# Inverting the delta rule's triangular blocks as 64x64 tiles, with the outer blocks in the last level and one modulation vector in the recurrence

## The reference, cut to what matters

```python
def gated_delta_chunked(q, k, v, beta, g):
    G = jnp.cumsum(gc, axis=-1)
    L = jnp.exp(jnp.where(incl, G[..., :, None] - G[..., None, :], -jnp.inf))
    kb = kc * bc[..., None]
    A = jnp.where(strict, jnp.einsum('bnhtd,bnhsd->bnhts', kb, kc) * L, 0.0)
    T = lax.linalg.triangular_solve(eye + A, eye, left_side=True, lower=True, unit_diagonal=True)
    U = T @ (vc * bc[..., None])
    W = T @ (kb * jnp.exp(G)[..., None])
    qk = jnp.where(incl, jnp.einsum('bnhtd,bnhsd->bnhts', qc, kc) * L, 0.0)

    def step(state, inp):
        v_new = u - w @ state
        o = qd @ state + qkc @ v_new
        state = gl[..., None, None] * state + jnp.swapaxes(kd, -1, -2) @ v_new
        return state, o
```

## Time and profile before

| | |
|---|---|
| median of three runs | 3473.8 us |
| the profiled execution | 3486.42 us, span 3484.6 us |
| TensorE busy (matmuls) | 3113.0 us, 89% |
| VectorE busy | 1155.4 us, 33% |
| ScalarE busy | 896.8 us, 26% |
| delta rule of layer 0 | 320.9 to 468.9 us |
| delta rule of layer 1 | 1177.6 to 1327.1 us |

### The profile page before, as it was taken

The page is one execution under the profiler, slowest core; times in us unless marked ns, Lnnn a source line. Parts: engine busy times, 40 slices in busy tenths (PEclk is TensorE's granted clock), DMA queues, the critical chain, the costliest instruction groups (busy, mean ns, idle before and its releaser), DMA issues. The chain is left out here.

```text
span 3484.6 us, 39509 instructions
## 1 busy us (share of the span) xinstructions
PE 3113.0 (89%) x17446; PEld 2112.2 (61%) x17446; DVE 1155.4 (33%) x1616; ACT 896.8 (26%) x1354; POOL 0.2 (0%) x4
## 2 busy tenths in 40 slices
PE   5997889999898788999989998879899985999997
PEld 3775767888676576788867766644343352443442
DVE  3446533233445653323343236630000136100002
ACT  3443223222444312322243350220000032100001
POOL 0000000000000000000000000000000000000000
PEclk8997989999999798999999999889999997999999
DMA  7224312322223411232363106249999952799996
GB/s 256 80 90 147 97 37 85 97 91 91 76 85 109 168 39 40 93 97 91 100 216 122 37 3 240 73 152 404 409 408 409 409 193 93 301 409 409 409 408 242
DMA packets 247386, 637.14 MB, mean 183 GB/s; under 512 B 12848, under 2 KB 110128, under 8 KB 247088
## 3 DMA queue, kind: packets, MB, share of 16 engines
q1 hardware_dynamic: 244128, 627.22, 48.4%
q10 hardware_dynamic: 3088, 7.40, 0.6%
HBM read 632.48 MB, written 2.10 MB: 182 GB/s over the span
## 5 line engine op out<-in xcount | busy, mean ns | idle before, releaser
L609 PE MATMUL ps<-mix_halves,work_halves 128*128 128x512 f32 (+1 forms) x1544 | 623.5, 404 | 39.5 <-DVE h_halves L2095 30.3
L609 PE MATMUL ps<-h_halves,work_halves 128*128 128x512 f32 (+1 forms) x1544 | 610.1, 395 | 4.6 <-DVE mix_halves L2095 2.4
L609 PE MATMUL ps<-mix_halves,ring_halves 128*128 128x512 f32 x1448 | 568.1, 392 | 0.0
L2095 DVE TENSOR_TENSOR ring_halves<-ring,work_halves 128x2048 fp32r<-128x2048 f32 (+2 forms) x125 | 252.6, 2021 | 546.2 <-ACT work_halves L1488 449.3
L609 PE MATMUL ps<-ring,work 128*64 128x512 f32 x1680 | 389.4, 594 | 22.3 <-DMA ring<-in_w_exp_gate 18.3
L609 PEld LDWEIGHTS ps<-mix_halves,work_halves 128*128 128x128 f32 (+1 forms) x1544 | 291.8, 189 | 126.7 <-issue 42.6
L609 PEld LDWEIGHTS ps<-h_halves,work_halves 128*128 128x128 f32 (+1 forms) x1544 | 292.5, 189 | 72.5 <-issue 6.4
L609 PEld LDWEIGHTS ps<-mix_halves,ring_halves 128*128 128x128 f32 x1448 | 272.3, 188 | 60.7
L1488 ACT ACTIVATE work_halves<-ring 128x2048 fp32r<-128x2048 f32 x102 | 188.3, 1846 | 425.6 <-PE ps L609 333.2
L609 PEld LDWEIGHTS ps<-ring,work 128*64 128x64 f32 x1680 | 128.0, 137 | 256.0 <-issue 255.6
L2474 DVE SCALAR_TENSOR_TENSOR x<-ps,small,x 128x512 f32<-128x512 f32 x112 | 82.3, 750 | 594.3 <-PE ps L609 592.8
(11 more groups left out here) (371 smaller groups left out, 3349.3 us busy)
## 6 DMA issues: line engine op xcount, KB each, us to landing
ring<-in_w_exp_gate SPq DMA_DIRECT2D x114, 1024.0 KB, 11.3
ring<-in_w_exp_down SPq DMA_DIRECT2D x100, 1024.0 KB, 12.8
ring<-in_w_exp_up SPq DMA_DIRECT2D x96, 1024.0 KB, 15.1
ring<-in_ada_w SPq DMA_DIRECT2D x48, 1024.0 KB, 7.4
ring<-in_w_mod SPq DMA_DIRECT2D x48, 1024.0 KB, 7.5
proj<-in_w_exp_up SPq DMA_DIRECT2D x28, 1024.0 KB, 12.8
proj<-in_w_exp_down SPq DMA_DIRECT2D x28, 1024.0 KB, 16.0
ring<-in_w_in SPq DMA_DIRECT2D x22, 1024.0 KB, 5.4
```

The lines of the kernel that those rows point to most:

```text
L609: i = pe.matmul(o, lhsT, rhs, start=start, stop=stop, **kw)
L2095: to("lo", tt(rounded(v), v, rounded(hi), ALU.subtract))
```

## The change

The 16 matrices are cut into 64x64 blocks. Only the diagonal ones are inverted by levels: the upper left blocks lie in partitions 0 to 63 and the lower right ones in partitions 64 to 127 of the same columns (`g_Ac`, `g_Tc`, `g_Yc`, `g_Xc`, 16 blocks side by side, 1024 elements to a partition where there were 2048). A product of a level is now 32 products of 64x64 by 64 columns, alternately in the upper left and the lower right quarter of the array (`products`). There are five full levels, up to blocks of 64. The last level forms the outer block alone from the right half of A (`g_Ar`): X = A T of the upper left inverse, 16 products, and X^T Y, 16 products. VectorE lays the result out as the full `g_Y` that the recurrence reads. Signals, copies and subtractions go by half (8 blocks) and no longer by head, each with 512 elements to a partition. The masks come from `b_mask`, 64 wide, left by the stage before. ScalarE has a new copy of the lower diagonal blocks (`g_diag`). Turning Y is now a product with the identity.

Modulation vector 5 moves into the recurrence: two panels after chunk 0, two after chunk 1, its turn after chunk 2, VectorE's `columns_out` after the loop.

```diff
@@ TensorE, delta
-                for i in (4, 5):
-                    for first in (0, 2):
-                        mod_panels(PLANS[f"layer{l}"], i, first, i, (4,))
+                for first in (0, 2):
+                    mod_panels(PLANS[f"layer{l}"], 4, first, 4, (4,))
                 pe.wait_ge(*due("g_y"))
...
+                def products(bank, lhs, rhs, half, signal):
+                    for g in blocks(half):
+                        for r in (lower, upper):
+                            mm(at_block(r, bank, g), lhs[r, g, :], rhs[r, g, :], True, True,
+                               signal if g % 8 == 7 and r is upper else None)
...
+                for n in range(len(LEVELS) - 2):
                     for half in range(2):
                         pe.wait_ge(*due("g_al"))
+                        if n:
+                            pe.wait_ge(*due("g_tt"))
+                        products(0, g_al[n % 2], g_Tc, half, "g_x")
                     if n == 0:
-                        pe.wait_ge(*due("mod_ready", 2))
+                        pe.wait_ge(*due("gn"))
+                        pe.wait_ge(*due("mod_ready"))
                     for half in range(2):
+                        pe.wait_ge(*due("g_x_sb"))
+                        if n:
+                            pe.wait_ge(*due("g_yt"))
+                        products(6, g_Yc, g_Xc, half, "g_dt")
+                        products(4, g_Xc, g_Yc, half, "g_dy")
+                for half in range(2):
+                    pe.wait_ge(*due("g_tt"))
+                    for g in blocks(half):
+                        mm(at_block(upper, 0, g), g_Ar[lower, g, :], g_Tc[lower, g, :], True, True,
+                           "g_x" if g % 8 == 7 else None)
+                for half in range(2):
+                    pe.wait_ge(*due("g_x_sb"))
+                    pe.wait_ge(*due("g_yt"))
+                    for g in blocks(half):
+                        mm(at_block(lower, 4, g), g_Xc[upper, g, :], g_Yc[upper, g, :], True, True,
+                           "g_dy" if g % 8 == 7 else None)
...
+                    if c < 2:
+                        mod_panels(PLANS[f"layer{l}"], 5, 2 * c, 5)
+                    if c == 2:
+                        mod_turn(5, 5)
@@ ScalarE, delta
+                act.wait_ge(*due("g_acc", 2))
+                to("g_diag", f(g_Ac[64:P, :, :], g_Ar[64:P, :, :], ACT.Copy))
...
+                for _ in LEVELS[1:-1]:
+                    for half in range(2):
+                        copy_half("g_x", g_Xc, half)
+                for half in range(2):
+                    copy_half("g_x", g_Xc, half, slice(64, P))
@@ VectorE, delta
+                for half in range(2):
+                    dve.wait_ge(*due("g_score", 2))
+                    s, d = (by_halves(v[:, 2 * half:2 * half + 2, :]) for v in (ps, g_L))
+                    tt(g_Ac[0:64, eight_of(half), :], s[0:64, :, 0, :], d[0:64, :, 0, :], ALU.mult)
+                    to("g_acc", tt(g_Ar[:, eight_of(half), :], s[:, :, 1, :], d[:, :, 1, :], ALU.mult))
...
-                link(tt(by16(g_A), by16(g_A), const("below").unsqueeze(1).to_broadcast([P, 16, P]), ALU.mult))
-                link(tt(by16(g_Y), by16(g_A), table(first_t, "level1").unsqueeze(1).to_broadcast([P, 16, P]), ALU.mult))
-                to("g_y", tt(by16(g_Y), ident.unsqueeze(1).to_broadcast([P, 16, P]), by16(g_Y), ALU.subtract))
+                dve.wait_ge(*due("g_diag"))
+                link(tt(g_Yc, g_Ac, b_mask[:, 6:7, :].to_broadcast([P, 16, 64]), ALU.mult))
+                to("g_y", tt(g_Yc, b_mask[:, 0:1, :].to_broadcast([P, 16, 64]), g_Yc, ALU.subtract))
...
+                dve.tensor_copy(g_Yq[0:64, :, 0, :], g_Yc[0:64, :, :])
+                dve.tensor_copy(g_Yq[64:P, :, 1, :], g_Yc[64:P, :, :])
+                for half in range(2):
+                    dve.wait_ge(*due("g_dy"))
+                    to("g_yt", ts(g_Yq[0:64, eight_of(half), 1, :], change(4, half)[0:64, :, :], -1.0, None, ALU.mult))
...
                 due("g_state")
+                columns_out(PLANS[f"layer{l}"], 5, 5)
                 coefficients(l)
```

More of the change, by code:

```diff
@@ L247 @@
     "g_kb": "VectorE: k beta", "g_k": "TensorE: k by tokens", "g_k_sb": "ScalarE: in SBUF",
+    "g_diag": "ScalarE: the lower diagonal blocks beside the upper ones",
     "g_score": "TensorE: a head's products", "g_acc": "VectorE: with decay", "g_y": "VectorE: the first level's inverse",
@@ L381, in build @@
         b_s, b_tmp = cut(work, 5120, 256, b=2, e=P), cut(work, 5376, 256, b=2, e=P)
-        g_A, g_T, g_Y = (four(work, 2048 * i) for i in range(3))
-        g_X = four(proj_all, 2048)
+        g_Ac, g_Ar, g_Tc, g_Yc = (cut(work, 1024 * i, 1024, g=16, t=64) for i in range(4))
+        g_Xc, g_Y = cut(proj_all, 2048, 1024, g=16, t=64), four(work, 4096)
+        g_Yq = g_Y.rearrange("p h (c u t) -> p (h c) u t", u=2, t=64)
         g_vt, g_kdt = cut(proj_all, 4096, 1024, c=4, f=256), cut(proj_all, 5120, 1024, c=4, f=256)
@@ L387, in build @@
         g_qk, g_L = four(hbuf, 0), four(hbuf, 2048)
-        g_al = (four(proj_all, 0), g_L)
-        g_eg = two(proj_all, 0)
+        g_al = (cut(proj_all, 3072, 1024, g=16, t=64), cut(hbuf, 2048, 1024, g=16, t=64))
+        g_eg = two(proj_all, 1024)
         g_s = cut(work, 7168, 256, b=2, e=P)
@@ L964, in delta @@
                 pe.wait_ge(*due("g_k_sb"))
-                for i in (4, 5):
-                    for first in (0, 2):
-                        mod_panels(PLANS[f"layer{l}"], i, first, i, (4,))
+                for first in (0, 2):
+                    mod_panels(PLANS[f"layer{l}"], 4, first, 4, (4,))
                 pe.wait_ge(*due("g_y"))
-                for hd in range(H1):
-                    for c in range(NT):
-                        turn(ps[:, hd, c * P:c * P + P], g_Y[:, hd, c * P:c * P + P], "g_t" if c == NT - 1 else None)
+                lower, upper = slice(0, 64), slice(64, P)
@@ new lines, in at_block, with blocks @@
+                def at_block(rows, bank, g):
+                    return ps[rows, bank + g // 8, g % 8 * 64:g % 8 * 64 + 64]
+                def blocks(half):
+                    return range(8 * half, 8 * half + 8)
+                def products(bank, lhs, rhs, half, signal):
[3 more added lines that the diff above has]
+                               signal if g % 8 == 7 and r is upper else None)
@@ L972, in delta @@
+                for g in range(16):
+                    for r in (lower, upper):
+                        t = pe.matmul(at_block(r, 0, g), g_Yc[r, g, :], ident[r, r], start=True, stop=True)
+                        if g % 8 == 7 and r is upper:
+                            t.then_inc(sem["g_t"], 1)
                 mod_turn(4, 4)
-                mod_turn(5, 5)
-                pe.wait_ge(*due("g_t_sb", H1))
-                for n, s in enumerate(reversed(LEVELS[:-1])):
-                    last = s == LEVELS[0]
+                pe.wait_ge(*due("g_t_sb", 2))
@@ L996, in delta @@
-                        if not last:
-                            if n == half == 0:
-                                pe.wait_ge(*due("gn"))
-                            for hd in (2 * half, 2 * half + 1):
-                                if half:
-                                    pe.wait_ge(*due("g_tt"))
-                                for c in range(NT):
-                                    cs = slice(c * P, c * P + P)
-                                    mm(ps[:, 6 + hd % 2, cs], g_Y[:, hd, cs], g_X[:, hd, cs], True, True,
-                                       "g_dt" if c == NT - 1 else None)
@@ L1006, in delta @@
-                    pe.wait_ge(*due("g_yt", 2))
-                    if not last:
-                        pe.wait_ge(*due("g_tt", 2))
+                        pe.wait_ge(*due("g_x_sb"))
[8 more added lines that the diff above has]
+                           "g_x" if g % 8 == 7 else None)
@@ L1742, in delta @@
                         split_panel()
+                    if c == 2:
+                        row_out(5, 5)
+                act.wait_ge(*due("mod_tr", 6))
                 act.wait_ge(*due("g_ds", NT))
@@ L2347, in hc @@
                     return v.rearrange("p (h c) -> p h c", c=4)
+                dve.memset(g_Yq[64:P, :, 0, :], 0.0)
                 dve.wait_ge(*due("g_gates_sb"))
```

79 lines of the change are left out of this document (33 added, 46 removed).

## The result

The changed kernel takes 3375.4 us (median of four executions, 3371.2 to 3381.4) against 3477.2 of the kernel before beside it: a ratio of 0.971, 95% interval 0.969 to 0.973. The forecast was 3432.0. The time lies inside the range given, 3372 to 3444, but the gain is more than twice what the likeliest case had; it is the first rival's case, *full clock*, which was put at 3379 with a chance of 0.24.

The account below looks back on a forecast made before the run. TensorE was taken to bound the kernel, with VectorE binding at the front of the two changed stages. Terms -5.1, -5.1, -14.2, -0.7 and +4.2 gave -20.9 us a layer, -41.8 for two: 3432.0 us, range 3372 to 3444.

Parts of the forecast that it names:

- the likeliest case: Levels start at clock 0.50 and stay there until the recurrence: -20.9 us a layer, 3432.0 us in all, chance 0.60.
- full clock: Rival: two quarters at once suffice for clock 1.00, a middle level takes 5.75 us; -47.3 us a layer, 3379 us; chance 0.24.
- burst: Half a level product, 32 instructions of 64x64 by 64: 0.94 us at clock 1.00, 1.71 us at 0.50.
- pairing: In the levels' products, two opposite quarters of the array work at once; doubted because both write one PSUM bank.
- The clock: From the gap before the first level until the recurrence, granted clock 0.50, a level taking 10.3 us.
- Front: Before the first X^T Y: fewer and smaller VectorE mask and block operations, after waiting for two heads; -5.1 us a layer.
- First level: From the first X^T Y: 11.9 us becomes four halves at 1.71, 6.8 us; -5.1 us a layer.
- four levels: Middle levels: 55.4 us becomes 41.2, at 10.3 a level, with no other engine binding; -14.2 us a layer.
- Last level: Four single-quarter bursts at 1.71 us plus latency, negation and clearing: 8.96 us becomes 8.2; -0.7 us a layer.
- Recurrence: Vector 5's panels lengthen two chunks and the start is at clock 0.50: +4.2 us a layer, between +1 and +7.
- Cost nothing there: At the front, before the change, vector 5's panels stood under VectorE's masks and cost no time.
- No pairing: Rival: hardware takes the quarters in turn, a level takes 20.5 us; +26.8 us a layer, 3527 us; chance 0.08.

Follow-up runs that it names:

- the kernel with one row half: Changed kernel, but both blocks of each pair in the middle levels' products take the lower rows and go to the two column halves by turns: 3412.8 us, ratio 0.981.
- one row half after the other: Changed kernel, but in each half product of the middle levels all eight lower-row blocks stand first, then all eight upper-row blocks: 3471.8 us, ratio 0.998.

## Why the prediction was wrong

- *What bounds the kernel, burst, pairing.* Right. A half product is 0.93 us at 1.00 (0.94 forecast) and 1.71 at 0.50, the figure forecast, measured in the kernel with one row half. Two readings were off. That "no row of this trace has opposite quarters at once" is wrong: the burst at 270.80 goes to all four quarters in turn and has 64 instructions in 1.16 us, so pairing deserved less doubt. And "next to no traffic: 58 GB/s" is a mean over the stage: from 342.9 to 362.7 us the loads run at 254 GB/s, and it is behind such loads that TensorE later paused.
- *The clock: the step that failed.* "A fully busy TensorE does not by itself bring the clock back" held, 78 busy us at 0.50. "One that addresses half of its array did not" was read wrongly off: those 64-row blocks lack half of the rows (eight instructions in one row half, then eight in the other for the next head), and I carried it over to two quarters as a half of the *area*. Two opposite quarters lack nothing of the rows. The kernels above part the two: one row half 0.50 for 53 us, one row half after the other 0.50 for 78 us, both row halves by turns back at 1.00 after 3.4 us. The levels took 5.8 us in place of 10.3. The sentence for the rival, that alternating quarters keep all rows in turn, was the mechanism, and it got 0.24.
- *Front* -5.4 for -5.1: right, by the same operations (the 0.55 us of waiting for two heads in the forecast's sum lie ahead of where the table starts; like for like it is -5.4 for -5.65). *First level* -6.9 and *four levels* -32.2 for -5.1 and -14.2: all the clock's. No other engine binds. *Last level* -3.8 for -0.7, likewise: 5.1 us, at 1.00.
- *Recurrence* +0.7 in layer 0 and -4.1 in layer 1 for +4.2: the sign of the move was wrong, too. The +4.2 doesn't follow from its own terms: 1.4, 2.1 and 1 are 4.5 before "a bit less than another slow chunk" is added. The first chunk came as priced, 10.6 us (8.53 and 2.1). But the 7.12 us that the sum took for a chunk at full clock has a slow stretch in it, the row below; at 1.00 a chunk without panels takes 5.76 us.

```profile
441.80:445.10 3.30, 3.14 (x20) 2.52 (x20) 0.65 (x2) 1.46 (x3) 0.00 (x0) 0.50 0.00 0
```

- *The panels in it* cost 0.6 us a chunk at 1.00 (6.4 against 5.8 of the third), but with them the clock stays up for longer; alone, the move makes the recurrence 3.2 and 4.5 us shorter. "Cost nothing there" was also incomplete: at the front the panels, used up early, pull loads into the levels. The kernel before had loads there too (352 GB/s in its first level) and no such pause; it used up a packet of instructions in 16 to 20 us, the changed one in 3.7.
- *The rivals.* Full clock is right to 4 us in the total, and in layer 0 term by term; in layer 1 its recurrence is off by 4.6 us. No pairing is out. The range held the result only because it was drawn out to this rival. The forecast asked at which clock the recurrence would start, and not what the moved work does to it.

## What to carry to other kernels

Where a clock decides, ask which rows of the array are at work, and not only how much of it: here small blocks on both row halves by turns were at full clock, and a row half by itself stayed at half clock for 53 us though TensorE never idled. Work that fills TensorE's short waits in a chain may be worth more than it costs. Many small instructions make TensorE depend on its instruction stream: keep large loads out of such a stretch, look for the cause of a pause ahead of it and not beside it, and look at what a removed wait used to cover.

## What the hardware showed that was not expected

- Two products of 64x64 run side by side (29 ns each at 1.00, 53 at 0.50) when they take opposite quarters, two row halves on one column half, or one row half's two column halves; row halves in one PSUM bank or in two make no difference.
- TensorE's instructions come by DMA, in packets of 16 KB (`q8 instruction`, 0.02 MB each). In the levels one comes about every 3.7 us (six in the 22.4 us from 356.9 in the changed kernel, in which TensorE ran 1527 instructions, some 255 a packet). Behind or beside loads of 350 GB/s TensorE stops for 0.8 to 2.9 us. The Trainium skill's page "Runtime: NRT & Kernel Launch" (section "Instruction fetch mechanics") has the cost of such a 16 KB block as mostly hidden; the trace agrees where nothing is loaded (25.89 us busy of 26.00, at 68 instructions a microsecond), and doesn't behind full DMA queues.
